# A new order of VectorE's sums and modulation pieces, and other waits for the second FFN products, in a float32 kernel of two transformer blocks on one core

## The reference

```python
cond = silu(c)
for i in range(2):
    mod = cond @ w_mod[i] + b_mod[i]                       # 6 vectors of 1024
    sh_m, sc_m, gt_m, sh_f, sc_f, gt_f = split(mod, 6)
    h = rms_norm(x, norm_mix_g[i]) * (1 + sc_m) + sh_m
    x = x + gt_m * (recurrent_mixer(h) if i == 0 else pool_mixer(h))
    h = rms_norm(x, norm_ffn_g[i]) * (1 + sc_f) + sh_f
    u = relu(h @ ffn_w1[i])                                # 1024 -> 4096
    x = x + gt_f * ((u * u) @ ffn_w2[i])                   # 4096 -> 1024
x = rms_norm(x, final_norm_g)
```

## Time and profile before

| | us |
|---|---|
| median of 3 runs | 2730.44 |
| lowest and highest run | 2724.49, 2734.41 |
| the profiled execution | 2725.24 |
| its span in the trace | 2723.4 |
| TensorE busy | 2532.5 |
| VectorE busy | 1140.0 |
| ACT busy | 479.0 |

### The profile page before, as it was taken

One profiled execution on the slowest core, in us unless ns is written; L12 is line 12 of the kernel. 1 busy time (PEld: TensorE's weight loads), 2 busy tenths in 40 slices (PEclk: granted clock), 3 DMA queues, 4 the chain that ended last, 5 costly groups with the idle time before them and its releaser, 6 DMA issues.

```text
span 2723.4 us, 26784 instructions
## 1 busy us (share of the span) xinstructions
PE 2532.5 (93%) x10975; PEld 1525.4 (56%) x10975; DVE 1140.0 (42%) x1926; ACT 479.0 (18%) x998; POOL 124.2 (5%) x232
## 2 busy tenths in 40 slices
PE   8999999999899999999969998898999969998898
PEld 4468888888788888455533333333555533333333
DVE  4765667655656644235551221112135551221112
ACT  2432121002222002124510000001124510000000
POOL 1320000100000000010000000000000000000000
PEclk9999999999999999999989999999999989999999
DMA  9633753651334234120349999999020349999997
GB/s 335 210 108 119 235 172 106 213 167 49 108 124 124 62 80 139 60 105 22 123 165 377 403 406 413 414 418 410 22 100 24 124 163 372 404 402 412 412 419 316
DMA packets 181545, 601.76 MB, mean 221 GB/s; under 512 B 8832, under 2 KB 123184, under 8 KB 156848
## 3 DMA queue, kind: packets, MB, share of 16 engines
q1 hardware_dynamic: 163392, 544.59, 52.5%
q0 software_dynamic: 16736, 51.20, 5.8%
q10 hardware_dynamic: 1296, 4.25, 0.4%
HBM read 593.72 MB, written 6.29 MB: 220 GB/s over the span
## 4 chain that ended last, share of the span: by engine, by line
PE 73%; DMA 20%; DVE 5%; issue 2%; ACT 1%; SPq 0%; POOL 0%; DVEq 0%; ACTq 0%
DMA arena<-in_w_down 18%; PE ps L1939 10%; PE ps L2499 8%; PE ps L2064 7%; PE ps L2511 6%; PE ps L2175 5%; PE ps L2423 4%; PE ps L1952 3%; PE ps L2169 3%; PE ps L1910 3%; PE ps L1810 2%; PE ps L1859 2%; PE ps L1834 2%; PE ps L1977 2%; PE ps L2188 2%; PE ps L2343 2%
## 5 line engine op out<-in xcount | busy, mean ns | idle before, releaser
L2499 PE MATMUL ps<-arena 128*64 128x512 f32 x2048 | 457.2, 599 | 29.7 <-DMA arena<-in_w_up 27.9
L2499 PEld LDWEIGHTS ps<-arena 128*64 128x64 f32 x2048 | 149.0, 138 | 321.7 <-issue 268.6
L2511 PE MATMUL ps<-arena 128*64 128x512 f32 x1024 | 243.2, 632 | 49.7 <-DMA arena<-in_w_down 48.3
L1939 PE MATMUL ps<-arena 128*128 128x256 f32 x1280 | 277.2, 379 | 2.0 <-issue 2.0
L1939 PEld LDWEIGHTS ps<-arena 128*128 128x128 f32 x1280 | 242.9, 190 | 35.6 <-issue 2.8
L2511 PEld LDWEIGHTS ps<-arena 128*64 128x64 f32 x1024 | 84.8, 145 | 205.6 <-issue 203.9
L2064 PE MATMUL ps<-arena 128*128 128x256 f32 x896 | 193.6, 379 | 0.0
L2064 PEld LDWEIGHTS ps<-arena 128*128 128x128 f32 x896 | 170.2, 190 | 23.1
L1952 PE MATMUL ps<-arena 128*128 128x256 f32 x672 | 154.7, 393 | 10.1 <-issue 3.7
L1952 PEld LDWEIGHTS ps<-arena 128*128 128x128 f32 x672 | 132.5, 198 | 30.4 <-issue 9.4
L1730 DVE TENSOR_SCALAR arena<-ps,arena 128x512 f32<-128x512 f32 x32 | 22.6, 746 | 275.4 <-PE ps L2511 275.4
(11 more groups left out here) (417 smaller groups left out, 2966.1 us busy)
## 6 DMA issues: line engine op xcount, KB each, us to landing
arena<-in_w_gate SPq DMA_DIRECT2D x64, 2048.0 KB, 44.2
arena<-in_w_up SPq DMA_DIRECT2D x64, 2048.0 KB, 40.1
arena<-in_w_down SPq DMA_DIRECT2D x64, 2048.0 KB, 38.9
arena<-in_ffn_w SPq DMA_DIRECT2D x24, 2048.0 KB, 9.8
arena<-in_w_mod POOLq DMA_DIRECT2D x80, 512.0 KB, 5.2
arena<-in_ffn_w SPq DMA_DIRECT2D x32, 1024.0 KB, 7.4
arena<-in_w_in SPq DMA_DIRECT2D x10, 1536.0 KB, 10.7
arena<-in_w_mod SPq DMA_DIRECT2D x4, 2048.0 KB, 19.9
```

Of the source, the lines that this page charges most:

```text
L1939: ins = mm(ps[:, i % 6, 0:256], src[:, k, P * j:P * j + P], x[:, k, :], start=(k == 0), stop=(k == 3))
L2499: ins = mm(ps[CAP * half:CAP * half + CAP, bank, :], xsT[:, 4 * q + k, :], wv[:, k, 512 * half:512 * half + 512], start=(q == 0 and k == 0 ...
L2511: ins.append(mm(ps[CAP * par:CAP * par + CAP, YE_BANK[half], :], hT2[par][:, k, CAP * q:CAP * q + CAP], w[par][0][:, k, 512 * half:512 * h ...
```

## The change

- 16 pieces (56 to 71) move from the second products into the mix loop of layer 0, which now does two a round; the numbers of `mod_columns` and `mod_sum` move with them. The other eight are placed one by one.
- `weight_sum(1, 0)` moves ahead of the short sums of p = 0.
- `F2A_BANK` is shifted by two, and in layer 1 the first two banks are exchanged. The first second product of a layer no longer waits for the whole of u (`u_free`), but for round 14 of the mix loop (`mix_done` + 90), whose last product had its bank. The full wait moves to the second product.
- The load of block 6 is awaited after product (2,1) instead of before it. Product (2,3) waits for one more copy of ACT.
- Seven of the eight squares and six of the seven sums of part 5 move ahead of the norm of part 4.
- In layer 1 the row sums of the first weight block move from steps 6, 7, 9, 12 to 12, 13, 14, 15.

```diff
-        SUMS_AT, ROWS_AT = ((4, 5, 7, 8), (13, 14, 15)), ((10, 11, 13, 14), (6, 7, 9, 12))
+        SUMS_AT, ROWS_AT = ((4, 5, 7, 8), (13, 14, 15)), ((10, 11, 13, 14), (12, 13, 14, 15))
...
-        F2A_BANK = [n % 6 for n in range(24)] + [2]
+        F2A_BANK = [(n + 2) % 6 for n in range(22)] + [2, 3, 4]
...
-        MOD_AT = {(0, 11): 5, (0, 19): 6, (0, 27): 7, }
+        MOD_AT = {(0, 11): 5, (0, 19): 6, (0, 22): 7, (0, 26): 8, (0, 30): 9}
...
-            for q in (3, 4):
-                squares(q)
-                root(q)
-                scaled(q)
-            squares(5)
+            squares(3)
+            root(3)
+            scaled(3)
+            squares(4)
+            squares(5, range(KC - 1))
+            root(4)
+            scaled(4)
+            squares(5, [KC - 1])
             ffn(1)
...
-                for i, bank in enumerate((0, 2)):
+                for i, bank in enumerate((2, 0)):
...
                     if l == 0:
-                        mod_piece(40 + m)
+                        mod_piece(40 + 2 * m)
+                        mod_piece(41 + 2 * m)
...
+            mod_piece(75)
+            made(0, 7)
+            weight_sum(1, 0)
             chain(V.tensor_tensor(ua[1], ua[0], made(0, 7), add))
...
             square_sum(4, KC - 1)
+            for k in range(1, KC - 1):
+                square_sum(5, k)
             mean_square(4)
             normed(4)
             whole(24, 1, 7)
-            for k in range(1, KC):
-                square_sum(5, k)
+            square_sum(5, KC - 1)
             ffn_first(1)
...
-                pe.wait_ge(sm["u_free"], U_BASE[l] + 48)
-
...
+            pe.wait_ge(sm["mix_done"], MIX_BASE[0] + 90)
             layer_product(0, 1, wx[:, 0:2048], u_b11)
-            mod_sum(8)
+            mod_sum(10)
+            pe.wait_ge(sm["u_free"], U_BASE[0] + 48)
             sums_in(0, 1)
...
-            mod_sum(9)
...
-            mod_sum(10)
+            mod_sum(11)
...
-            wx, wy = landed(("f2", 0, 2)), landed(("f2", 0, 6))
+            wx = landed(("f2", 0, 2))
             x_is(13)
             layer_product(2, 1, wx[:, 0:2048], u_b11)
             x_is(1)
+            wy = landed(("f2", 0, 6))
             layer_product(2, 4, wy[:, 2048:], u_t24)
...
-            mod_sum(11)
...
+            pe.wait_ge(sm["q_sb"], 6)
             sums_in(2, 4)
...
+                if p == 0:
+                    pe.wait_ge(sm["mix_done"], MIX_BASE[1] + 90)
...
-                ffn_product(wx[:, 0:2048], u_b11, 0)
+                ffn_product(wx[:, 0:2048], u_b11, 2)
```

More of the change, by code:

```diff
@@ L1243, in upper_right @@
                 to_x(p, 1, ua[0]).then_inc(sm["x_done"], 1)
-            def pieces(n):
-                for _, i in zip(range(n), PIECES):
-                    mod_piece(i)
             def whole(n, half, c):
@@ L1277, in _ @@
             lower_right(0)
-            for n in range(4):
+            for n in range(1, 4):
                 weight_sum(1, n)
@@ L1281, in _ @@
             hidden_sum(4)
-            mod_columns(9)
-            pieces(2)
+            mod_piece(76)
             first_block(1)
-            pieces(3)
+            mod_piece(77)
             chain(V.tensor_tensor(ua[0], qa[0], made(1, 6), add))
@@ L1303, in _ @@
             weight_sum(2, 3)
-            mod_columns(10)
+            mod_columns(11)
             first_block(2)
-            pieces(2)
             chain(V.tensor_tensor(ua[0], qa[0], made(2, 6), add))
```

17 lines of the change are left out of this document (7 added, 10 removed).

## The result

The changed kernel takes **2697.9 us** (median of 4 runs, 2695.95 to 2699.11) against 2731.11 (4 runs, 2724.49 to 2734.41): a ratio of 0.9881, 95% interval 0.9861 to 0.99. The forecast was 2699.0, so it was right. Its profiled execution took 2697.01 us, with a span of 2695.2.

What follows compares the result with a forecast made beforehand. TensorE was taken to bound the kernel, busy 2532.5 of 2723.4 us. Idle times of 19.9 plus 9.7 us of half clock, less 0.5, gave 29.1 us of gain: 2696.1 or 2701.3, so 2699 us; range 2691 to 2710.

Steps and rivals of the forecast that it cites:

- hidden_sum(1): Start of second products: its value ready at 456.6, wanted by TensorE at 457.5, so the 1.41 us idle time goes.
- hidden_sum(5): Layer 0's second products: one piece stands before it, product (1,5) covers both, so the 2.60 us idle time goes.
- The row sums: Layer 1, blocks 12 to 15: at most 3.4 us a block against 3.5, cost taken as 0; the 5.93 gap goes.
- The piece in the even rounds: Layer 0's mix loop: wanted at 381.4, its transfer lands at about 381.0, just in time.
- Block 6: Second products: load of 12.3 us against 15.6 of TensorE work, so the 3.71 us wait goes with 3.3 to spare.
- weight_sum(1,0): Second products: directly behind made(0,7), covered by product (1,1), so the 2.33 us idle time goes with 1 to 2 spare.
- The gap of 2.55 us: Layer 1, before norm(5): six of seven sums run earlier, so the gap goes, or at worst 0.3 us stays.
- Waits for in_w_mod in the mix loop: Sign in VectorE's piece groups: waits under 0.5 us fit the forecast, over 1.5 us mean (b).
- (b): Pieces land late in the mix loop, 8.7 instead of 6.6 us: 4.2 to 9.8 us more, 2703 to 2709; chance 0.14.
- (a): TensorE still falls to 1.2 GHz at a short wait, or one gap forms again: some 6 us, 2705; chance 0.14.
- (c): Slower: mix-loop piece landings use up the gain at 12.6 us; 2733 and more profiled, 2740 as median; chance 0.02.
- (d): Gain does not get through: expert stage paced by its own transfers, nothing arrives, 2730; chance 0.03.

## Why the prediction was right

**The sum.** Predicted: 29.6 us of gaps and slow matmuls go, less 0.5. Measured in the stages: 30.3 and 31.1. By stage: the second products gave 20.4, where 2.33 + 3.1 + 2.60 + 1.8 + 3.71 + 3.0 = 16.5 and two mod_sum moved out at 1.7 us make 19.9; layer 1's first products gave 10.6 against 2.55 + 5.93 + 1.8 = 10.3; layer 1's mix loop gave 1.6 against 1.41. The mix loop of layer 0 took 2.2 us more, where two mod_sum at 1.70 less 1.58 (below) are 1.8. So the loop paid 0.3 us for its 16 pieces; I had taken 0.5. The run with the pieces put back says the same: its loop is 3.7 us shorter, of which 3.4 are the two mod_sum. My test for being wrong there (over 2 us beyond the two mod_sum) is far from met.

Most of what the stages give beyond the sum is one small term that the prediction left out. Where TensorE runs on, a row starts 0.14 to 0.17 us before the row ahead of it has ended (450.30 + 1.84 = 452.14 against 452.00, and 443.29 + 7.17 = 450.46 against 450.30 in the earlier trace rows). Behind a bracket it does not, so a break costs its bracket and that much more. Seven breaks are some 1.1 us: 0.5 of the second products, 0.3 of layer 1's first products, 0.2 of its mix loop (1.41 + 0.17 = 1.58 against 1.57 measured).

**How close the total is, is partly luck.** The gain was put at 29.1 us on the scale of one profiled execution; the two profiled executions differ by 28.2, the stages by 30.3 and 31.1, the medians by 33.2. The term left out above (1.1 us too little) and some 3 us that the second network gave back (below) lean against each other, and the 2699 was placed between two readings of the level of before, 2696.1 and 2701.3. That the mechanism holds is shown by the stages; that the median came within 1.1 us of the forecast is not a measure of it.

**Which part brought what.** Putting back one at a time costs 8.1 (pieces), 2.1 (block 6), 7.9 (row sums), 3.5 (waits, both layers) and 4.4 (squares): 26.0 us. The 5.6 us that are missing to 31.6 are the interplay of pieces and block 6, shown by the run with both. This is within 0.5 to 1.3 us of the measured difference. The match is looser than it looks: 1.9 us of the 31.6 are half clock behind norm(5), which before did not have, and the half clock with the pieces put back is 1.7 us where before had 4.9. Part by part the cause is shown; in sum the account is good to some 3 us.

**Steps that were right.** hidden_sum(1) and the early start of the products held in both layers, though in layer 1 with 0.15 us of a gap left at 874.05 (L1393), a margin that I had not worked out there. hidden_sum(5) no longer stalls TensorE. The row sums cost nothing at blocks 12 to 15. The piece in the even rounds came just in time, as worked out: issued at 374.9, it took 6.4 us, and VectorE, which wants it at 381.33, does not wait. That its start of 381.43 agrees with the 381.4 of the prediction to a tenth is luck: the changed kernel's loop began 1.25 us earlier, one more mod_sum (1.7) stands ahead of it, and the piece before it took 0.75 us instead of 1.28.

**Steps that were off.**
- *Block 6.* I compared 12.3 us of landing with 15.6 of cover and put the whole 6.7 us down to the order of the wait. The 12.3 was itself a number of the kernel before, with three pieces in flight; the change takes these away and the landing falls to 10.0. The term was right as a part of the sum, since both causes go, but the order of the wait alone is worth 2.1 of it. The cover was better than thought: 5.6 us to spare and not 3.3.
- *weight_sum(1,0).* "Directly behind made(0,7)" left out that the sum reads the weight block, which landed at 496.3. The move brought nothing (the run with the old place), and the margin that I gave as 1 to 2 us is 0.2; without the 1.8 us that the load was late it would have been 2.0. What removed the stall of 2.33 us is the pieces' departure: the run with the old place has no stall either.
- *The gap of 2.55 us.* It was entered without half clock, as the trace of before had it. With it back in the changed kernel the same gap cost 1.9 us more. As before has none of it in two profiled executions, the sum was not hurt.
- *Waits for in_w_mod in the mix loop.* I named under 0.5 us as the mark of the forecast and over 1.5 as that of rival (b). Two waits of 0.71 and 1.28 us came, between the marks; one fell into a round with a mod_sum and neither reached TensorE.

**The rivals.** (a) did not come, but was nearer than its 0.14 said in one place, 0.2 us; even then its price would have begun at 0.18 us, as in the run with the full waits, and not at 6, because a short gap costs itself only. (b) did not come: the landings that mattered in the loop were 6.4 us, with 7.7 as the longest there. (c) asked for 12.6. (d) did not come either: the first gather of the expert stage starts 31.5 us earlier (1.25 of it ahead of layer 0's mix loop, where the kernels do not differ).

```profile
1423.50 0.98 POOL L2628 DMA_INDIRECT arena<-xn_rows,get_c  x1 [0.28 <-POOL get_c L2626]
```

```profile
1392.04 0.98 POOL L2627 DMA_INDIRECT arena<-xn_rows,get_c  x1 [0.28 <-POOL get_c L2625]
```

**What stays open.** The spans differ by 28.2 us and not by 31.5: the second network gave some 3 us back. In the two profiled executions of before the part behind layer 1's mix loop took 1832.0 and 1831.5 us; in the twelve of changed kernels it took 1830.0 to 1840.3, mostly more than before. The part ahead of layer 0's mix loop, in which no kernel differs, varies from 298.7 to 303.2 by itself. The rows tell where it goes. From the first gather of the first expert stage to that of the second it took 815.85 us before and 817.24 in the repeat of before; 821.58 and 821.96 in the two executions of the changed kernel; and 818.5 to 822.7 in all twelve of changed kernels. Between layer 1's mix loop and this stretch, and behind it, the two kernels agree within their spread (532.1 against 532.2 and 532.3 us; 484.1 and 482.2 against 481.6 and 484.1). First before, then changed (columns as in the earlier trace rows):

```profile
1423.50:2239.35 815.85, 738.92 (x3195) 336.97 (x3195) 241.22 (x490) 135.53 (x297) 18.28 (x34) 0.97 0.68 273
```

```profile
1392.04:2213.62 821.58, 747.30 (x3195) 338.53 (x3195) 241.31 (x490) 135.76 (x297) 18.28 (x33) 0.96 0.68 271
```

TensorE is busy 8.4 us longer for the same 3195 matmuls, at a lower mean granted clock. So the loss is there and goes with more time at half clock. It is also why TensorE's busy time in the whole span fell by 6.4 us only, when up to the end of layer 1's mix loop it had fallen by 11.9 (854.28 to 842.34). My step "a gain in the two FFNs goes one for one to the end" is shown up to the first gather; behind it the gain shrinks by some 3 us. Why there is more of it, and whether the change causes it, no run here was made to tell: before has two profiled executions only.

The Trainium skill ("DMA: Bandwidth & Descriptors", section Queues, rings and completion order) has each DMA engine alternate between queues, packet by packet, from which the prediction inferred that pieces slow the weight loads rather than themselves. This case agrees with the first half of that inference where the loads are large: a 2 MB block took 10.0 to 10.3 us without and 12.3 to 14.3 with a group of pieces beside it. It does not agree with the second half: a piece took 4.2 us with little beside it (issued at 514.89) and 6.4 to 8.7 beside the weight loads, so both sides slow down. In the mix loop the 1 MB loads took 7.6 with two pieces and 7.5 with one, so there it does not show.

## What to carry to other kernels

When a stall ends on a load, ask what else was in flight: a transfer time that is read from the kernel before belongs to the traffic of before, and a change that moves the neighbours changes it too. Two causes of one stall are only seen when both are put back together; one at a time would have left 5.6 of 31 us without an owner. And before an operation is moved up, look for the last of its inputs, not for the one that the reorder is about.

## What of the hardware was not expected

The price of an idle time in TensorE's clock does not follow from its length. All of these are from TensorE's timelines; the slow part is the duration of the row behind less 0.217 us a matmul (0.1 to 0.2 us of it is the end of the row and stands behind every break). The last column is half of TensorE's busy time in the stretch behind the gap in which the granted clock was 0.50, the 1.2 GHz level.

| place | gap, us -> slow part behind it, us | half of the busy time at 0.50, us |
|---|---|---|
| first weight sums or short sums of the second products | 2.33 -> 3.1, 2.84 -> 3.0 (before); 3.73 -> 1.5, 3.21 -> 2.1 (pieces put back) | 3.0, 3.0; 1.4, 2.0 |
| hidden_sum(5) | 2.60 -> 1.8, 2.06 -> 1.9 (before); 2.85 -> 0.2, 2.18 -> 0.2 (pieces put back) | 1.6, 1.7; 0, 0 |
| block 6 | 3.71 -> 3.0, 4.61 -> 2.8 (before); 5.33 -> 2.7 (both put back); 1.68 -> 0.0 (block 6 alone) | 3.0, 2.8; 2.7; 0 |
| norm(5) | 2.55 -> 0, 2.54 -> 0 (before); 2.54 -> 1.9 (squares put back) | 0, 0; 1.7 |
| pool product | 5.93 -> 1.8, 5.86 -> 1.7 (before); 5.90 -> 2.0 (row sums put back) | 1.6, 1.5; 1.9 |

Three of these stretches, as windows (columns as in the earlier trace rows): behind the gap of 2.33 us before, behind the one of 3.73 us with the pieces put back, and behind the 2.54 us with the squares put back.

```profile
503.80:510.60 6.80, 5.99 (x14) 4.86 (x15) 6.59 (x4) 0.00 (x0) 0.00 (x0) 0.50 0.00 0
```

```profile
507.10:510.40 3.30, 2.82 (x7) 2.28 (x8) 3.27 (x4) 0.06 (x1) 0.00 (x0) 0.50 0.00 0
```

```profile
665.60:668.90 3.30, 3.30 (x10) 2.59 (x9) 2.22 (x3) 0.42 (x1) 0.00 (x0) 0.50 0.18 69
```

So the price is half of the time that TensorE works within the slow stretch, to 0.2 us in every row of the table. It depends on how long that stretch is and on how much of it falls into the gap itself, where it costs nothing. The stretch of before runs from 503.8 to 510.6 and TensorE starts in it at 504.61. With the pieces put back the clock falls only 3.2 us after the gap of 3.73 us began, and is back at 1.00 from 510.5 on: a longer gap at half the price.

What decides whether a stretch comes at all, and how long it is, was not found: 2.06 us had one where 2.85 had none, and a gap of 2.54 us had none or one. At the places of this table, gaps of 1.68 us or less cost no clock, and those of 3.2 us or more always did. Within one kernel the price repeats to 0.2 us even when the gap moves by 0.9. The position of the gap in time or the work ahead of it may decide, and no run here separates them.
